# A projection of both latent tiles, and the end of the block of expert slots that fell into its middle, put one behind the other

## The reference

```python
for l in range(DEPTH):                      # 2 layers
    h  = rmsnorm(x,  norm_attn_g[l]) * (1 + sc1)  + sh1
    hc = rmsnorm(xc, norm_attn_g[l]) * (1 + sc1c) + sh1c
    y, yc = parallel_mixers(h, hc, ...)      # h @ w_in -> q_d, k_d, v_d, c_q, c_kv -> attention -> w_out
    x = x + g1 * y
    x = x + g2 * peer_ffn(norm(x))           # the same for xc in layer 0

# peer_ffn, per token: 8 heads x 16 experts = 128 rows of peer_u and of peer_v
u = take(peer_u, eidx); v = take(peer_v, eidx)
act = gelu(einsum('ted,td->te', u, xb)) * gate
out = einsum('te,ted->td', act, v)
```

## Time and profile before

| | |
|---|---|
| Median of three runs | 2632.14 us (2626.13 to 2635.8) |
| The profiled execution, its own time | 2623.53 us |
| Its span in the trace | 2621.6 us |
| PE busy | 2067.3 us (79%) |
| DVE busy | 1832.3 us (70%) |
| ACT busy | 1119.5 us (43%) |
| POOL busy | 975.2 us (37%) |
| Moved by DMA | 980.25 MB, mean 374 GB/s |
| Chain that ended last | PE 32%, DVE 27%, DMA 22%, ACT 10%, issue 8% |

### The profile page before, as it was taken

The page is one execution under the profiler, slowest core; times in us unless marked ns, Lnnn a source line. Parts: engine busy times, 40 slices in busy tenths (PEclk is TensorE's granted clock), DMA queues, the critical chain, the costliest instruction groups (busy, mean ns, idle before and its releaser), DMA issues.

```text
span 2621.6 us, 26027 instructions
## 1 busy us (share of the span) xinstructions
PE 2067.3 (79%) x6888; PEld 1088.7 (42%) x6888; DVE 1832.3 (70%) x4176; ACT 1119.5 (43%) x3090; POOL 975.2 (37%) x916
## 2 busy tenths in 40 slices
PE   6997787777979876988677797878867988577766
PEld 2554444443435444444334343435543444333322
DVE  0147986995567779976979665644597787767776
ACT  2123474444236443744443723432244644333333
POOL 1012343332443433444343444320133443445453
PEclk8998898888998988989889898998988998888888
DMA  8588999997999999999999999994799999999997
GB/s 342 172 301 321 405 395 402 404 381 279 415 399 363 390 394 387 409 407 411 413 417 392 397 417 415 393 383 159 273 411 363 397 398 408 374 387 419 422 413 328
DMA packets 215704, 980.25 MB, mean 374 GB/s; under 512 B 17660, under 2 KB 75544, under 8 KB 117272
## 3 DMA queue, kind: packets, MB, share of 16 engines
q0 software_dynamic: 123648, 855.69, 80.1%
q1 hardware_dynamic: 91928, 123.05, 13.6%
HBM read 977.62 MB, written 1.05 MB: 373 GB/s over the span
## 4 chain that ended last, share of the span: by engine, by line
PE 32%; DVE 27%; DMA 22%; ACT 10%; issue 8%; POOL 1%; SPq 0%; POOLq 0%; DVEq 0%; ACTq 0%
DMA EXPERT<-in_peer_uv,FIX 19%; PE VS L1010 12%; PE PA L863 9%; DVE EXPERT L1630 9%; DVE ACC L1640 3%; DVE SCR L1264 2%; PE PA L891 2%; DMA WT<-in_peer_wq 2%; PE PB L787 2%; PE PB L1000 1%; PE VS L816 1%; ACT L1203 1%; PE PA L940 1%; PE PB L931 1%; ACT DIAG L1218 1%
## 5 line engine op out<-in xcount | busy, mean ns | idle before, releaser
L1010 PE MATMUL VS<-EXPERT,DIAG 128*128 128x512 f32 x2304 | 1170.4, 650 | 262.5 <-ACT DIAG L1218 261.8
L695 POOL DMA_INDIRECT EXPERT<-in_peer_uv,FIX x768 | 898.2, 1170 | 1088.4 <-PE VS L1010 739.1
L1630 DVE CUSTOM_DVE_ANT_0 EXPERT<-EXPERT,H 128x1024 f32<-128x1024 f32 x768 | 924.1, 1223 | 333.2 <-DMA EXPERT<-in_peer_uv,FIX 324.3
L1010 PEld LDWEIGHTS VS<-EXPERT,DIAG 128*128 128x128 f32 x2304 | 457.2, 209 | 840.9 <-issue 471.3
L1211 ACT ACTIVATE GEL<-DOT 128x1 f32<-128x1 f32 x768 | 155.2, 202 | 1046.6 <-DVE DOT L1630 1045.5
L863 PE MATMUL PA<-WT,HT 128*128 128x512 f32 (+2 forms) x720 | 294.5, 555 | 8.7 <-issue 5.4
L1640 DVE SCALAR_TENSOR_TENSOR ACC<-EXPERT,WEI,ACC 128x1024 f32<-128x1024 f32 x192 | 246.0, 1281 | 19.1 <-ACT WEI L1213 19.1
L1218 ACT ACTIVATE DIAG<-IDN,WEI 128x128 f32<-128x128 f32 x576 | 231.3, 402 | 60.0 <-PE VS L1010 41.9
L1000 PE MATMUL PB<-HT,WT 128*128 128x128 f32 (+1 forms) x1472 | 215.1, 308 | 35.1 <-issue 33.9
L1213 ACT ACTIVATE WEI<-GEL,GATE 128x1 f32<-128x1 f32 x768 | 226.3, 295 | 24.9
L1000 PEld LDWEIGHTS PB<-HT,WT 128*128 128x128 f32 x1472 | 207.8, 218 | 59.8 <-issue 57.2
(11 more groups left out here) (147 smaller groups left out, 1677.0 us busy)
## 6 DMA issues: line engine op xcount, KB each, us to landing
EXPERT<-in_w_ada POOLq DMA_DIRECT2D x48, 1024.0 KB, 11.9
WT<-in_peer_wq SPq DMA_DIRECT2D x92, 512.0 KB, 18.0
WT<-in_w_in SPq DMA_DIRECT2D x48, 512.0 KB, 10.0
WT<-in_w_out SPq DMA_DIRECT2D x48, 512.0 KB, 9.9
EXPERT<-in_peer_uv,FIX POOLq DMA_INDIRECT x768, 11.4
WT<-in_w_in SPq DMA_DIRECT2D x16, 384.0 KB, 9.8
WT<-in_w_in SPq DMA_DIRECT2D x16, 288.0 KB, 6.6
WT<-in_mla_wq_up SPq DMA_DIRECT2D x4, 512.0 KB, 10.0
```

Of the source, the lines that this page charges most:

```text
L695: pool.indirect_dma_start(out=EXPERT[:, j, :], out_offset=None, in_=a["peer_uv"], in_offset=bass.IndirectOffsetOnAxis(ap=FIX[:, par, j:j + ...
L1010: ins = nc.tensor.matmul(VSUM[n][:, :], DIAG[:, i, :], EXPERT[:, j, D + n * W:D + (n + 1) * W], start=first, stop=last_one)
L1630: nc.vector.tensor_tensor_reduce(out=EXPERT[:, j, 0:D], in0=EXPERT[:, j, 0:D], in1=H2[:, b % HB, :], scale=1.0, scalar=0.0, op0=ALU.mult, ...
```

## The change

`weave` gets four lines and a constant. Ahead of the first part of a projection of more than one tile it looks at the next eight entries of the stream. If a `close` is among them, all entries up to and with that close are put out first.

```diff
@@ -38,6 +38,7 @@
 GROUP = 32
 STAGED = (0, 1, 2, 4, 5, 6, 7)
 KEEP = 3
+STRADDLE = 8
 LATE_PIECE = len(STAGED)
@@ -252,6 +253,11 @@
     for n, s in enumerate(background):
         for c in needed(s):
             while c not in seen:
+                step()
+        if s[0] == "in" and s[5] == 0 and len(s[4]) > 1:
+            soon = [c for c in stream[at:at + STRADDLE] if c[0] == "close"]
+            while soon and soon[0] not in seen:
+                assert picked(stream[at])
                 step()
         out.append(s)
         done += cost(s)
```

## The result

The changed kernel takes 2612.25 us in the median (2605.44 to 2618.64), the kernel before 2629.84 beside it on the same chip. The ratio is 0.9944, with a 95% interval of 0.9924 to 0.9964: some 15 us less, in the interval 9 to 20. The medians differ by 17.6.

The account below looks back on a forecast made before the run. DMA at 414 GB/s was the ceiling where slots run, with a whole-machine stop at block 0's end. PE 14.1 us and DMA 13.5 or 14.7 earlier were taken as 14: 2632.1 - 14.0 = 2618.1 us, range 2609 to 2629.

Parts of the forecast that it names:

- The chances: Whole kernel: faster 0.51, same 0.43, slower 0.04, with 13.2 us as what a measurement can tell from no change.
- PE's sum: PE from the end of block 0, step by step: `kd` starts at 636.1 against 650.18, 14.1 us earlier.
- new wait of about 1 us for the second PA bank: Ahead of `qd`, PE idles until DVE's gate product frees the bank at 617.2, about 1 us.
- second way to the sum, by the waits: Check on PE: three waits 11.1 us plus half clock 5.3, less new waits 1.8 and 0.4, makes 14.2 us.
- the cover: Block 1's dot products behind the rotations end by 639, PE wants the first at 644.7: 5 us spare, no cost.
- One gap of 2.2 us: DMA idles from 631.5 until the ninth gather's bytes at 633.7; otherwise it gains 13.5 us by share, 14.7 by bytes.
- DMA's number is the one that is carried on: Next stage: DVE waits 24 times, 31.1 us, for gathers, so DMA's gain of 13.5 or 14.7 us counts.
- The clock falls in the new waits: Rival: PE's short gaps before the projection halve its clock, at most 2.6 us lost, gain 11.5, 2620.6 us; chance 0.12.
- The gain is given back: Rival, 650 to 740 us: PE waits for diagonals, 2 us each; three waits give 8 us, 2624 us; chance 0.16.
- Weights too late: Rival: `kd`'s second piece lands over 20.5 us after issue; at 48 us, 13.4 us slower, 2645.5 us; chance 0.04.
- The sign that I named as wrong: Listed as refuting: PE waiting for a weight piece behind 636, clock 0.5 within `qd`, or trace distance shrinking after 740 us.
- no clock time is fixed further down that could take it back: Behind the changed place the machine goes on 14 us earlier in the same state, until the end.

Follow-up runs that it names:

- late products: Changed kernel plus three extra rounds of products (12 matmuls, 5.2 us of PE) ahead of the first part of projection `vd`; ratio 0.9973 to the kernel before.
- two loads: Changed kernel with 5.2 us of extra PE products ahead of `vd`, and separately with four 512 KB memory copies; ratio 0.9973 each to the kernel before.
- kernel with slot 0 early: Changed kernel with block 1's first slot on PE between the projection's second and third parts, not third and fourth; ratio 0.9947 to the kernel before.
- longer close: Changed kernel with four extra DVE writes of the gate diagonal between the halves of block 0's close; ratio 0.9977 to the kernel before.
- run with four copies: Changed kernel with four 512 KB memory-to-memory copies issued by SP behind the second piece of `vd`; ratio 0.9973 to the kernel before.

## Why the prediction was right, point by point

**The size.** 2618.1 us was forecast and 2612.25 measured, inside the range of 2609 to 2629. The forecast was a gain of 14 us on the median then known, 0.53%; the three ratios of the changed kernel give 0.56, 0.67 and 0.50%. Of the 5.9 us between 2618.1 and 2612.25, 2.3 are the kernel before, which had 2632.14 when I wrote and 2629.84 beside this run (2624.15, 2620.59 and 2622.73 later on); the other 3.6 are what the difference of the medians has above 14, within the spread of single executions. The chances had set the line between faster and the same at 13.2 us. The measured 15 us lie above it, the interval of 9 to 20 reaches to both sides, so the run does not settle that line. The profiled execution was to take 2609.5 us and took 2618.64; of its end more below.

**PE's sum.** `kd` at 636.1 was forecast, 14.1 us earlier; it came at 636.70, 13.5 earlier, or 13.8 when the 0.3 us are taken off by which slots 100 to 119 already lie later. Gate rows at 613.5 were forecast and came at 613.87. The new wait of about 1 us for the second PA bank is the 0.88 in front of `qd`, and the 0.8 between the gate rows is 0.78. DVE's product was to start at 616.5 and started at 616.90, so the lateness of the gate rows is handed on, and 0.16 us lie between its end at 617.59 and the projection, which my sum had at nothing. All behind it is on time: three parts, slot 0, the fourth part and two slots take 18.95 us, and 18.9 were counted. The prediction's second way to the sum, by the waits, had one term too large: it put the gate rows at the half clock at 1.2 us more for each set. The rows give 1.0 (2.08 against 1.05 and 1.16), and with that the second way comes to 13.8 us and not 14.2.

**DVE and POOL.** The rotations wait 3.65 us (3.5 forecast) until 631.75 (631.0). The eighth gather is issued at 616.76 (617), the ninth at 631.37 (631). PE waits for none of the last dot products of the first eight, so the cover held.

**DMA.** One gap of 2.2 us was to stay. By share 21.1 x (1 - 0.94/1.02) = 1.7 us are left, by bytes 21.1 x (1 - 347/414) = 3.4. The gain is 14.0 us by share and 13.5 by bytes; 13.5 and 14.7 were forecast.

**"DMA's number is the one that is carried on"** stands in size and was too narrow as a reason. I argued it from DVE's waits for gathers. The late products show that 5.2 us of PE work are handed on too, 3.8 us of them at slot 152. PE and DMA are both near the limit, and here the gain came on both, 13.8 us on PE and 13.5 to 14.0 on DMA. That a gain on only one of them would have brought next to nothing follows from the two loads but is not shown: no run takes time from one alone, and in the kernel with slot 0 early DMA's idle time hardly shrank.

**The rivals.** *The clock falls in the new waits* did not happen in the profiled execution, PEclk being 1.00 in both stretches. But I held it for all or nothing, a property of the order. It is a matter of the single execution: one of eight traces shows it, and it cost 1.7 us where I had bounded 2.6. The bound itself was too low: behind the longer gap of the longer close the same projection took 3.0 us more, and the gate rows 0.9. The Trainium skill, "TensorE: Matmul & The Clock Gate", section "A second HAM failure mode: psum-queue depth-cycling", describes clock swings from frequent short idles between groups of matmuls. The run with four copies agrees with it (12.23 us instead of 10.54), while the seven others don't. My ground against it, the like place at the close of block 2, was a single sample, and the sign that I had named for this rival, a clock of 0.5 within `qd`, came in the run with four copies. *The gain is given back* between PE and DMA behind 650 us: no, -13.8 us at slot 136 is -13.3 at slot 160 and -13.6 at slot 384. *Weights too late*: no wait in the changed kernel; the mechanism exists and costs 14.19 us when 4.2 MB are put ahead of the pieces.

**The sign that I named as wrong** was "a distance between the traces that shrinks after 740 us". It did shrink, to 4.7 us at slot 512, and by my own list that would have spoken against me. The list was wrong here. The repeated kernel before shows a jump of this size with no edit. The layer boundary has two lengths some 5 us apart that go with the granted clock in the attention. The sentence "no clock time is fixed further down that could take it back" holds for the order of the program, but one pair of executions cannot show it. At slot 384 the three traces of the changed kernel stand at -13.6, -13.4 and -10.3 us; at slot 767 at -5.2, -10.3 and -14.9, and against the second trace of the kernel before at -7.9, -12.9 and -17.6. So the forecast that the end comes 14 us earlier holds for no single pair with certainty; the repeated runs carry the gain, not the ends of the traces.

**What stays open.** What decides in an execution which clock the attention gets, and whether the two gaps at the close bring the clock down, I can't say. Nothing that I found in the rows ahead of these places tells the two kinds apart. What moves the distances of the changed kernel by up to 7 us within layer 1 was not followed up. Nor was a version found that is measurably faster than the changed kernel; slot 0 early is as fast.

## What to carry to other kernels

When one engine's in-order queue holds a step that waits for a long stage of another (here the rotation for the projection), look for what is queued behind it and is asked for by everyone: put that in front, and let the long stage run in the time that it takes. Work out the gain on each full resource separately, for where two are level the smaller gain is the one to count on, and count the waits that the new order opens. Judge it near the change by the distance to a point where both are full, and at the end by repeated runs with the unchanged kernel among them: one pair of traces can be 5 us off by a stage that has nothing to do with it.

## What the runs showed that I had not expected

The same instructions with the same gaps on PE (0.79 and 0.89 us, light gate rows between) ran at the full clock in seven executions and at 0.72 over 6 us in one. The attention between the layers took 39 us at a clock of 0.87 or 44 us at 0.73, with no edit. Copies of 4.2 MB on the queue of the weights cost not some 10 us but about 15, and PE waited 14.19 us for a piece behind them, while 2.1 MB cost about their own time of reading and no wait for a piece. From the end of DVE's product with the first gate to the start of the projection, which waits for its bank, lie 0.16 us in every one of the nine traces of the changed kernel and its variants that keep this order.
